# One kernel, four regroupings: slot table from one-hot products with eight weight units asked ahead, and three stages of the second block

## The reference

```python
# first block
sh1, sc1, g1, sh2, sc2, g2 = split(silu(c) @ w_ada + b_ada, 6)
h = rms_norm(x, norm1_g) * (1 + sc1) + sh1
q, k, v, u = split(h @ w_in)                   # 4 heads x 2 x 64, rotary on q, k
a_out = diff_attention(q, k, v, lam)           # softmax(s0) - lam * softmax(s1)
p_out = multiscale_pool(u)                     # windows 2, 4, 8, 16
x = x + g1 * (concat(a_out, p_out) @ w_out)
h = rms_norm(x, norm2_g) * (1 + sc2) + sh2
g_sel = argmax(h @ w_rg + b_rg)                # one of 4 groups
e = top2(softmax((h @ w_re + b_re)[g_sel]))    # 2 of its 8 experts
y[tok] = sum(w_e * (silu(h @ w_gate[e]) * (h @ w_up[e])) @ w_down[e])
x = x + g2 * y;  x = rms_norm(x, final_g)
# second block, per layer (2 layers)
cols = rms_norm(x) @ w_in
y_gdn  = gated_delta_rule(conv(q, k, v), decay, beta)   # 6 heads, both directions, chunks of 64
y_mla  = softmax(q_mla @ k_mla.T * 96**-0.5) @ v_mla    # 6 heads
y_rwkv = rwkv7(shifted r, k, v, w, a)                   # 4 heads, both directions
x = x + (concat(y_gdn, y_mla, y_rwkv) * silu(gate)) @ w_out
```

## Time and profile before

| | |
|---|---|
| median of 3 runs | 2225.78 us (2225.41 to 2228.92) |
| profiled execution | 2220.6 us, span 2218.4 us, mean granted PE clock 0.947 |
| PE busy | 84% |
| DVE, ACT, POOL busy | 35%, 27%, 10% |
| DMA | 303.54 MB, mean 137 GB/s |

### The profile page before, as it was taken

How to read it: one execution, slowest core, us unless ns; L and a number is a source line. 1 busy time by engine, 2 the same in 40 slices (tenths; PEclk the granted TensorE clock), 3 DMA queues, 4 the chain that set the end, 5 groups by cost and what they waited for, 6 DMA issues and landing times.

```text
span 2218.4 us, 45669 instructions
## 1 busy us (share of the span) xinstructions
PE 1866.7 (84%) x18488; PEld 1069.3 (48%) x18488; DVE 777.7 (35%) x1445; ACT 591.2 (27%) x994; POOL 223.8 (10%) x273
## 2 busy tenths in 40 slices
PE   5999983877777775799998889979899997899887
PEld 2444532444444442357765853344358756743443
DVE  1233424111111111536556731350455557522431
ACT  3014521000000000334315423250243244232331
POOL 0002213111111110001003000001001012000001
PEclk9999996999999998899999999999999999899999
DMA  9563022999999996220000012100110000031101
GB/s 354 203 240 121 7 81 71 389 421 422 420 413 417 420 425 258 94 69 31 3 2 2 4 66 67 62 1 29 66 67 4 3 2 2 3 118 38 39 1 38
DMA packets 72048, 303.54 MB, mean 137 GB/s; under 512 B 8860, under 2 KB 20364, under 8 KB 54848
## 3 DMA queue, kind: packets, MB, share of 16 engines
q1 hardware_dynamic: 62240, 287.49, 32.8%
q0 software_dynamic: 5872, 9.68, 1.3%
q10 hardware_dynamic: 3760, 3.85, 0.5%
HBM read 296.67 MB, written 12.71 MB: 139 GB/s over the span
## 4 chain that ended last, share of the span: by engine, by line
PE 71%; DVE 11%; another core or an unknown queue 7%; ACT 5%; issue 3%; DMA 1%; ACTq 1%; DVEq 0%; POOLq 0%; SPq 0%; POOL 0%
PE bank L2070 11%; PE bank L458 11%; PE bank L2086 5%; PE bank L935 5%; PE bank L487 5%; PE bank L480 4%; PE bank L1912 3%; PE bank L2008 2%; PE bank L906 2%; DVE arena L1423 1%; ACT arena L947 1%; PE bank L1947 1%; PE bank L920 1%; PE bank L1934 1%
## 5 line engine op out<-in xcount | busy, mean ns | idle before, releaser
L2070 PE MATMUL bank<-arena 128*64 128x256 f32 x2048 | 241.4, 391 | 85.8 <-remote 85.8
L458 PE MATMUL bank<-hT,arena 128*128 128x512 f32 (+1 forms) x640 | 294.7, 617 | 13.1 <-DVE hT L2630 7.7
L2070 PEld LDWEIGHTS bank<-arena 128*64 128x64 f32 x2048 | 150.6, 140 | 189.0 <-issue 130.0
L480 PE MATMUL bank<-arena 64*64 64x64 f32 x6656 | 213.9, 220 | 22.6 <-DVE arena L1546 7.4
L480 PEld LDWEIGHTS bank<-arena 64*64 64x64 f32 x6656 | 202.6, 135 | 36.6 <-DVE arena L1546 10.5
L458 PEld LDWEIGHTS bank<-hT,arena 128*128 128x128 f32 (+1 forms) x640 | 124.7, 197 | 177.9 <-issue 160.4
L2578 DVE COPY arena<-bank 128x256 f32<-128x256 f32 x32 | 13.6, 425 | 377.5 <-PE bank L2078 377.5
L2086 PE MATMUL bank<-arena 128*64 128x512 f32 x512 | 118.6, 605 | 17.3 <-remote 17.3
L947 ACT ACTIVATE arena<-bank 128x512 f32<-128x512 f32 (+3 forms) x146 | 86.2, 591 | 157.3 <-PE bank L458 92.3
L487 PE MATMUL bank<-hT,arena 128*128 128x512 f32 x224 | 108.5, 622 | 16.5 <-ACTq L948 16.5
L935 PE MATMUL bank<-arena 128*128 128x512 f32 x256 | 110.4, 593 | 0.0
(11 more groups left out here) (413 smaller groups left out, 2562.9 us busy)
## 6 DMA issues: line engine op xcount, KB each, us to landing
arena<-w_gate SPq DMA_DIRECT2D x32, 2048.0 KB, 15.3
arena<-w_up SPq DMA_DIRECT2D x32, 2048.0 KB
arena<-w_down SPq DMA_DIRECT2D x32, 2048.0 KB, 11.3
arena<-w_ada SPq DMA_DIRECT2D x12, 2048.0 KB, 19.4
arena<-w_in SPq DMA_DIRECT2D x10, 2048.0 KB, 12.0
arena<-w_out SPq DMA_DIRECT2D x6, 2048.0 KB, 8.0
arena<-w_in SPq DMA_DIRECT2D x6, 1536.0 KB, 6.8
arena<-y_scratch SPq DMA_DIRECT2D x4, 1024.0 KB, 7.9
```

The lines of the kernel that those rows point to most:

```text
L458: m = pe.matmul(bank[b][lo:lo + w, :], slot2(n)[:, k, c:c + w], hT[:, k, :], start=(k == 0), stop=(k == KD - 1))
L480: m = pe.matmul(o[half(f), s, t], lhs[half(f), s, t], rhs[half(f), s, t], start=True, stop=True)
L2070: mm = pe.matmul(bank[b][c * CAP:(c + 1) * CAP, 0:FE // 2], XT[j][:, k % 4, k // 4, :], slot(ring_at + i)[:, k, c * (FE // 2):(c + 1) * (F ...
```

## The change

The kernel after is one kernel with these edits:

1. Start: the cosines and sines, `pool_w` and the router weights are asked for by ACT behind `mod_moved(3)`; DVE and PE wait for them where they first use them.
2. Router: the second norm's gain and shift are multiplied into the router weights (`w_gain`, `w_shift`), and the eight products w_gain x xT stand between the projection's last four tiles; `rs` scales the logits afterwards. POOL makes six of the eight tiles of hT. The rotary arguments and their sines move into the projection, the positions' request ahead of attention.
3. Slot table: each of the 1024 choices has a one-hot of its place in a block (64) and of its block (47, times three fields); 16 PE products add them up to the table in PSUM, DVE copies it to `info`. The DRAM table, its scatters and reads go. POOL gathers a constant block without a copy.
4. Weights: expert 0's gate and up go to other SBUF areas (`early`), the ring's six slots take 0's down, 1's three and 2's gate and up.
5. GDN: PE makes only the cumulative sums; DVE adds the keys' term and takes a minimum with the far constant; ACT's exponential is in place. The first pair's sums move ahead of column 8; the DVE chain runs direction by direction.
6. RWKV: the z products run inside the recurrence, in banks 6 and 7, which four products with zeros open; the outputs keep the state's part.
7. MLA: the scale is in the move of q, DVE's maximum is negated by the reduction, values stand one iteration later and ahead of the transpositions.

```diff
+            late_cols = CN["cosA"][0]
+            act.dma_start(c_sb[:, 0:late_cols], cn[:, 0:late_cols]).then_inc(sem("params_loaded"), 16)
             act.dma_start(r1[:], row1.to_broadcast([P, N_R1])).then_inc(sem("params_loaded"), 16)
-            act.dma_start(pool_w[:], w_pool[0].rearrange("g c d -> c g d")).then_inc(sem("pool_w_loaded"), 16)
-            act.dma_start(w_router[:, :, 0:4], w_rg[0].rearrange("(k p) n -> p k n", p=P)).then_inc(sem("router_loaded"), 16)
-            act.dma_start(w_router[:, :, 4:36], w_re[0].rearrange("(k p) n -> p k n", p=P)).then_inc(sem("router_loaded"), 16)
...
+            act.dma_start(c_sb[:, late_cols:], cn[:, late_cols:]).then_inc(sem("pool_w_loaded"), 16)
+            act.dma_start(pool_w[:], w_pool[0].rearrange("g c d -> c g d")).then_inc(sem("pool_w_loaded"), 16)
+            act.dma_start(w_router[:, :, 0:4], w_rg[0].rearrange("(k p) n -> p k n", p=P)).then_inc(sem("router_loaded"), 16)
+            act.dma_start(w_router[:, :, 4:36], w_re[0].rearrange("(k p) n -> p k n", p=P)).then_inc(sem("router_loaded"), 16)
...
+            chain(dve.tensor_tensor(w_gain, w_router[:], over_cols(gs[:, 1, :]), ALU.mult))
+            chain(dve.tensor_tensor(w_shift, w_router[:], over_cols(mod[:, 24:32]), ALU.mult))
+            chain(dve.tensor_reduce(shift_sum.rearrange("p (n o) -> p n o", o=1), w_shift.rearrange("p k n -> p n k"), AX.X, ALU.add))
...
+            pe.matmul(bank[0][:, 0:36], ones, shift_sum, start=True, stop=True).then_inc(for_dve[0], 1)
             take(pe, slot_full[(out_at + 1) % SLOTS], 16)
             for i in range(4, KD):
                 take(pe, bank_free[i])
                 projected(i, 0, KD).then_inc(for_dve[i], 1)
+                if i == 4:
+                    take(pe, bank_free[0])
+                for k in (2 * (i - 4), 2 * (i - 4) + 1):
+                    pe.wait_ge(sem("x_mixed"), k + 1)
+                    mm = pe.matmul(bank[0][0:36, :], w_gain[:, k, :], xT[:, k, :], start=(k == 0), stop=(k == KD - 1))
+            mm.then_inc(for_dve[0], 1)
...
+            chain(dve.tensor_tensor(lgT, bank[0][0:36, :], rs[0:36, :], ALU.mult))
+            dve.sem_inc(bank_free[0], 1)
+            for k in range(2):
+                dve.scalar_tensor_tensor(hT[:, k, :], xT[:, k, :], gs[:, 1, k:k + 1], rs[:],
+                                         ALU.mult, ALU.mult).then_inc(sem("scaled"), 1)
...
+            pe.wait_ge(sem("h_ready"), 2 * KD)
+            turn_h(0)
...
+            take(pe, bank_free[0])
+            for n in range(2 * TT):
+                if n % TT == 0:
+                    pe.wait_ge(sem("choices_full"), 2 + n // TT)
+                for c in range(2):
+                    mm = pe.matmul(bank[0][c * CAP:(c + 1) * CAP, 0:3 * N_BLK], lo_hot[:, n, :],
+                                   fields[:, n].rearrange("p f b -> p (f b)"), start=(n == 0), stop=(n == 2 * TT - 1))
+            mm.then_inc(for_dve[0], 1)
...
+            chain(dve.tensor_scalar(block_no, at, 1.0 / CAP, -0.4921875, ALU.mult, ALU.add))
+            chain(dve.tensor_scalar(block_no, block_no, MAGIC, None, ALU.add))
+            chain(dve.tensor_scalar(block_no, block_no, MAGIC, None, ALU.subtract))
+            chain(dve.scalar_tensor_tensor(place, block_no, -float(CAP), at, ALU.mult, ALU.add))
+            chain.mark(dve.tensor_tensor(lo_hot, over(place, CAP), steps_of(CAP), ALU.is_equal))
+            chain.mark(dve.tensor_tensor(hi_hot, over(block_no, N_BLK), steps_of(N_BLK), ALU.is_equal))
+            take(dve, sem("func_full"))
...
+            for k in range(2):
+                n = slice(TT * k, TT * k + TT)
+                shape = [P, TT, 3, N_BLK]
+                chain(dve.tensor_tensor(fields[:, n], hi_hot[:, n].rearrange("p n (o b) -> p n o b", o=1).to_broadcast(shape),
+                                        vals[:, n].rearrange("p n (f o) -> p n f o", o=1).to_broadcast(shape), ALU.mult))
+                dve.sem_inc(sem("choices_full"), 1)
+            take(dve, for_dve[0])
+            table = bank[0][:, 0:3 * N_BLK].rearrange("p (f b) -> p b f", f=3)
+            chain.mark(dve.tensor_copy(info[:, :, 2:3].bitcast(F32), table[:, :, 2:3]))
+            chain(dve.tensor_scalar(row_f, table[:, :, 0:2], no_row, None, ALU.add))
+            chain(dve.tensor_copy(info[:, :, 0:2], row_f))
+            dve.sem_inc(bank_free[0], 1)
...
+            pool.wait_ge(sem("rs_ready"), 6)
+            for k in range(2, KD):
+                pool.tensor_tensor(hT[:, k, :], xT[:, k, :], rs[:], ALU.mult).then_inc(sem("h_part"), 1)
...
-            for k in range(2):
-                for t in range(TT):
-                    pool.indirect_dma_start(
-                        slot_d, bass.IndirectOffsetOnAxis(ap=dest[:, k, t:t + 1], axis=0), rows[:, k, t, :], None,
-                        bounds_check=N_BLK * CAP - 1, oob_is_err=False).then_inc(sem("slot_table"), 16)
-            pool.wait_ge(sem("slot_table"), 16 + 16 * 2 * TT)
-            for c in range(2):
-                pool.dma_start(info[c * CAP:(c + 1) * CAP], slot_d.rearrange("(b s) c -> s b c", s=CAP)[:, :, 4 * c:4 * c + 4])\
-                    .then_inc(sem("slot_table"), 16)
-            pool.wait_ge(sem("slot_table"), 48 + 16 * 2 * TT)
...
+            weights_unit(2, 0, 0)
+            weights_unit(2, 1, 1)
+            weights_unit(0, 2, 2)
+            weights_unit(1, 0, 3)
+            weights_unit(1, 1, 4)
+            early_unit(0)
+            weights_unit(1, 2, 5)
+            sp.wait_ge(sem("h_stored"), 16 * TT)
+            early_unit(1)
+            weights_unit(2, 2, 2)
+            for i in range(3):
+                weights_unit(3, i, 3 + i)
+            with sp.Fori(0, N_EXP // 2 - 2) as pair:
                 for j in range(2):
-                    expert_weights(j, pair, 3 * j)
+                    expert_weights(j, pair + 2, 3 * j)
...
-                        for f in range(2):
-                            i64 = ident[half(f), half(f)]
-                            o = bank[d][half(f), :]
-                            pe.matmul(blocks(o), i64, over_blocks(const2("far" + name)[half(f)], CG), start=True, stop=False)
-                            start_of = g_c2[half(f), :, c:c + 2].rearrange("p t (s o) -> p s t o", o=1)
-                            pe.matmul(pieces(o), i64, start_of.to_broadcast([CG, 2, TT, CG]), start=False, stop=False)
...
+                        key_term = g_c2[:, :, c:c + 2].rearrange("p t (s o) -> p s t o", o=1).to_broadcast([P, 2, TT, CG])
+                        e_args[d].wait()
+                        chain(dve.tensor_tensor(pieces(g_V[d]), pieces(bank[b + d]), key_term, ALU.add))
+                        dve.tensor_tensor(blocks(g_V[d]), blocks(g_V[d]), over_blocks(const2("farF" if d == 0 else "farB")),
+                                          ALU.min).then_inc(sem(f"g_e_in{d}"), 1)
...
+                        chain(dve.scalar_tensor_tensor(two(g_Bn[d]), kk, -1.0, two(g_V[d]), ALU.mult, ALU.mult))
+                        chain(dve.tensor_tensor(blocks(g_Y[d]), blocks(g_Bn[d]), merged(d, 0, True).bitcast(F32), ALU.mult))
...
+                for f in range(2):
+                    for s in range(2):
+                        pe.matmul(bank[6 + f][half(s), :], blk[half(f), half(1 - f)], over_blocks(const2("I64")[half(f)], CG),
+                                  start=True, stop=False)
...
+                            keys_values(d, t, f, 0)
+                    if n > 0:
+                        values_within(8 * n, 8 * n + 4)
...
+                    values_within(8 * n + 4 if n > 0 else 0, 8 * n + 8)
+                    m = updates_within(n)
...
-                    if 3 <= i < n + 3:
-                        j = i - 3
-                        pe.wait_ge(sem("probs_ready"), j + 1)
-                        to_tokens(4 + j % 2, m_pr[:, j % 4, :])
-                    if i >= 5 and i % 2 == 1:
-                        p = (i - 5) // 2
+                    if i >= 6 and i % 2 == 0:
+                        p = (i - 6) // 2
...
-                        chain(dve.tensor_reduce(st[:, 2:3], bank[i % 4][:, :], AX.X, ALU.max))
-                        chain(dve.tensor_scalar(st[:, 0:1], st[:, 2:3], -QK_M ** -0.5, None, ALU.mult))
-                        dve.sem_inc(sem("maxima_ready"), 1)
+                        dve.tensor_reduce(st[:, 0:1], bank[i % 4][:, :], AX.X, ALU.max, negate=True).then_inc(sem("maxima_ready"), 1)
```

424 lines of the change are left out of this document (249 added, 175 removed).

## The result

| | before | after |
|---|---|---|
| median | 2225.6 us (2222.72 to 2228.92, four runs) | 2154.2 us (2149.62 to 2158.78, four runs) |
| span of the profiled execution | 2218.4 | 2150.1 |
| PE, DVE, ACT, POOL busy | 84, 35, 27, 10% | 86, 37, 27, 10% |

The ratio is 0.9685, 95% interval 0.9658 to 0.9712: 71 us less (64 to 76), where the forecast had 60 less and 2166.0. The range held it; the forecast itself was 12 us too slow.

What follows compares the result with a forecast made beforehand. PE bound most of the second block, the weights' stream the expert loop, a serial chain 340 to 375 us. −18.7 − 2 x (7.5 + 3 + 10) = −59.7 from 2220.6 gave 2161 profiled, 2166 median; range 2145 to 2198.

Steps and rivals of the forecast that it cites:

- MLA, −10 a layer: MLA tiles: the closed ring between engines opens, a pair takes 4.1 us instead of 5.13; −10 us a layer, ends −5 and −14.
- RWKV, −3 a layer: RWKV: within-chunk products move from the outputs into the recurrence; net −3 us a layer, ends −6 and +2.
- The recurrence's term: RWKV recurrence, per layer: the moved products add +1.5 to +3 us, the four zero starts 1.9 or less.
- Rival (d): Whole kernel: PE's granted clock falls and it gets slower than before; 2266 us with 100 us of matmul affected; chance 0.03.
- GDN, −7.5 a layer: GDN chunks: less PE work, −3.5 us in second and third pair, −0.5 to −1.7 in the first; ends −4 and −9.
- First block, −18.7: First block: −16.7 us from an earlier first expert product and −2 from the start; ends −10 and −24.
- half block: Start: the w_re request was taken to hold ACT's queue for half its 7.84 us; gain 2, ends −2.5 and +3.7.
- T + 6.6: Out-projection: its last product, ending at T = 310.75 us before, ends 6.6 us later through added DVE operations and router products.
- Rival (c): Slot table: POOL tiles and the shared port hold counts and one-hots; first expert product only 8 us earlier, 2174; chance 0.10.
- Eight units ahead: Expert weights: prefetching more units is worth 0, since the third request still waits for slot 2, 21.5 us behind first expert product.
- (a): Second block: regroupings bring little, the MLA ring closes elsewhere near 5 us and the recurrence repays RWKV's gain; 2192; chance 0.17.
- (b): Expert loop: the weights' stream starts two units of 5.3 us earlier, a further −10.6; 2155; chance 0.12.

Runs made afterwards that it cites:

- the experiment: Eight unread 512-column products a layer added where PE waits at the first GDN pair, against the kernel after; 2156.17 us, ratio 0.9679 to before.
- the order mended: Kernel after with weights requested in PE's order, including down of expert 30 ahead of gate and up of 31; 2149.36 us, ratio 0.9648 to before.

## Why the prediction was right, and where its terms were off

The sign, the range and the order of the parts were right. Four terms were off: MLA and RWKV gave more than their sums, GDN and the first block less, and the span fell by 68.3 us where the sum had 59.7. That the total came so near is in part luck: the errors have both signs.

**MLA, −10 a layer, was −16.** The mechanism is the forecast's: with L1660's step out of the ring and the values later, the waits are gone and PE's work bounds the pair. The term was mis-sized three times the same way. An undisturbed pair takes 3.77 us, where I had 4.1. Before's disturbed pairs, which I gave no gain of their own, gained more than the others: over the 24 maxima, 11.5 pairs apart, a pair takes 4.09 us instead of 5.35 in the first layer, and in the second the tiles fell from 63.7 to 46.5 us, 17.2 where I had 11 x 1.0. And the extra iteration that I charged cost nothing that shows. PE at 15.78 of 16 us in after's undisturbed stretch says what is late next: PE itself. This line is of the windows of after:

```profile
1441.00:1457.00 16.00, 15.78 (x116) 9.41 (x114) 11.29 (x27) 11.48 (x25) 0.00 (x0) 1.00 0.01 3
```

**RWKV, −3 a layer, was about −3.6 and −9.2.** The outputs' term was right: −6.8 forecast, −7.5 in both layers (136.3 and 135.2 us from the last step to the first MLA maximum before, 128.8 and 127.8 after). The recurrence's term was right for the layer that I had read. Rows 2 showed me the first layer's, at clock 1.00. There the six intervals went from 12.9 to 14.0 us, +1.1 (at that rate 1.5 for eight steps, the low end of my +1.5 to +3). From the wait to the second step, where the zero starts stand, it is 2.9 us more (4.4 against 1.6), with 1.9 forecast for the four products. Together +3.9, where the forecast had +3.4 to +4.9. What failed is that I took it for both layers. The second layer's recurrence ran at 1.2 GHz before: the six intervals went from 16.5 to 13.9, the start cost 0.9 more, together −1.7. One window of the second layer would have told me. Rival (d) had the cause right and weighed only one direction of it: a change can also move PE to the higher level.

**GDN, −7.5 a layer, was some −2.5 to −5.** Second and third pair gave −3.4 and −3.5 in the first layer and −3.5 and −3.9 in the second, as worked out from rows 9 (−3.5 each). The first pair gave +1.4 and −2.7, nothing clear, where I had −0.5 to −1.7. In the chain two DVE steps of 0.69 and 0.65 us take 1.06 and 0.99 beside POOL's products there, and the clock falls to 0.72; filling PE in the experiment took the clock's part away and gained nothing net. What the whole part is worth lies between the 5 us over two layers of the trace and the 9 of the medians, 11 of the ratios. Some of the pairs' gain is lost again, and the traces say where: behind the third pair. From its last inversion step to PE's wait ahead of the recurrence pass 156.1 and 157.0 us in before, 159.1 and 157.2 in after, and 156 to 161 in the other kernels. The kernel with the GDN part undone has 159.7 and 157.5 there as well, so the loss need not be the GDN part's. Its cause stays open.

**First block, −18.7, was −11.6.** Step by step:
- Start: −2.2 against −2, in a trace at the good end; the eleven traces with this start have a mean of −0.9 against the one of before. The half block that I took was 4.87 us of w_re (half of 7.84 is 3.9), and PE waited for ACT as feared.
- Attention and projection: the last product ends at 315.95, forecast 315.35 (T + 6.6 was the old 310.75 less the start's 2 and these 6.6). Right.
- rs stands 7.0 behind it (7 forecast), the logits 10.4 (9.2 forecast).
- Choices and counts: 21.0 behind it, forecast 18.8, ends 17.5 and 21. Rival (c)'s mechanism, POOL's products beside DVE's steps, at 3 us; (c) priced it so that the first expert product came only 8 us sooner. The rule of "SBUF — State Buffer" in the Trainium skill, section "Who interferes with whom", that I had weighed and left out of the sum, is borne out: 1.19 us beside POOL, 0.18 without it. By it I had worked out 2 to 4 us more for the routing, and the chain from logits to choices is 3.2 us over that of the kernel without POOL's products. The forecast held this in its bounds and not in the term; it belonged in the term.
- The table's last eight products took 3.1 us and not 1.8; the granted clock was 0.63 from 345 to 352. From the first gather to the first expert product pass 8.35 us where I had 9.1.
- First expert product −14.7, where the sum had −16.7 and 2 more for the start, −18.7: 0.6 us too late up to the projection's last product, 2.2 more up to the counts, the rest in the table.
- Eight units ahead: 0, as forecast, and by the forecast's reason, w_down's wait at slot 2, to 0.1 us.
- Behind the loop −2.4 are lost again: from the last scatter to the read of y pass 9.9 us (855.16 to 865.07) where before has 7.5 (869.84 to 877.31). The other kernels with the new form have 9.9 to 10.2 too, so it is no chance; no run here separates its cause, and it stays open.

**The rivals.** (a) is out by the undone MLA part. (b) is out for the order of requests that the change has. With the order mended 9.9 us come out, near its 10.6; six units ahead in the mended order were not run, so how much of the 9.9 the two extra units bring is not shown. (c) had the mechanism right and too much of it. (d) did not come: the mean granted clock is 0.95 in both kernels. In the recurrence of the second layer the change went the other way, from the lower level to the upper.
